# Two model blocks on one core: the second half of a layer as one block and one weight stream, and scatter steps in pairs

## The reference, cut to what matters

```
# end of the recurrent branch, per head of 64
y = (y - mean) * rsqrt(var + RW_GN_EPS) * lnx_g + lnx_b
y = (y + sum(r*k*r_k) * v) * g            # g = sigmoid(gd) @ g_up
# merge, output projection
proj  = einsum('bsgc,gcd->bsgd', branches, w_branch[l])        # 3 x 512 -> 1024
gates = sigmoid(gate_logits)                                   # 1024 -> 3 x 1024
x = x + sum(gates * proj, axis=2) @ w_out[l]                   # 1024 -> 1024
# feed-forward
u = rmsnorm(x, norm2_g[l]) @ ffn_w_up[l]                       # 1024 -> 5632
c = conv_b + sum_j conv_w[j] * shift(u, j)                     # width 3, causal
gate, val = split(c)
x = x + (silu(gate) * val) @ ffn_w_down[l]                     # 2816 -> 1024
```

## Time and profile before

| what | value |
|---|---|
| runs | 3702.34, 3706.68, 3707.23 us; median 3706.68 |
| profiled execution | 3699.1 us, its span 3697.3 us |
| PE busy | 3160.2 us (85%), 20284 instructions |
| weight loads | 2250.0 us (61%) |
| DVE, ACT, POOL busy | 1210.4, 1034.1, 1000.0 us (33%, 28%, 27%) |
| read from HBM | 398.22 MB |
| mean granted clock of TensorE | 0.925 |

### The profile page before, as it was taken

One profiled execution on the slowest core, in us unless ns is written; L12 is line 12 of the kernel. 1 busy time (PEld: TensorE's weight loads), 2 busy tenths in 40 slices (PEclk: granted clock), 3 DMA queues, 4 the chain that ended last, 5 costly groups with the idle time before them and its releaser, 6 DMA issues. The chain is left out here.

```text
span 3697.3 us, 50790 instructions
## 1 busy us (share of the span) xinstructions
PE 3160.2 (85%) x20284; PEld 2250.0 (61%) x20285; DVE 1210.4 (33%) x1819; ACT 1034.1 (28%) x1411; POOL 1000.0 (27%) x560
## 2 busy tenths in 40 slices
PE   6987799879997997979879998386866976999997
PEld 5767766668875776856668876265335855443442
DVE  2175411234401257421224420514652042222222
ACT  3442321144422343232134421221333221111111
POOL 2352123234441353123234442133001521100100
PEclk9998999989998998989999999688888987999998
DMA  3210112122222120012212220120001313898984
GB/s 125 75 57 6 40 69 85 62 81 101 100 94 79 69 74 16 4 71 85 74 70 101 91 105 32 46 80 16 0 23 57 114 40 145 365 394 365 394 358 192
DMA packets 54161, 402.61 MB, mean 109 GB/s; under 512 B 7280, under 2 KB 8432, under 8 KB 14704
## 3 DMA queue, kind: packets, MB, share of 16 engines
q1 hardware_dynamic: 54000, 400.34, 28.0%
HBM read 398.22 MB, written 2.10 MB: 108 GB/s over the span
## 5 line engine op out<-in xcount | busy, mean ns | idle before, releaser
L246 POOL TENSOR_TENSOR w_lo<-w,w_hi 128x1024 fp32r<-128x1024 f32 (+1 forms) x216 | 598.3, 2772 | 1340.3 <-ACT w_hi L241 1340.3
L241 ACT CAST w_hi<-w 128x1024 fp32r<-128x1024 f32 (+1 forms) x216 | 248.7, 1157 | 685.8 <-PE bank L273 647.5
L264 PE MATMUL bank<-h_hi,w_hi 128*128 128x512 f32 x1280 | 349.1, 416 | 63.6 <-ACT w_hi L241 63.6
L264 PEld LDWEIGHTS bank<-h_hi,w_hi 128*128 128x128 f32 x1280 | 244.3, 191 | 144.3 <-ACT w_hi L241 52.0
L273 PE MATMUL bank<-h_hi,w_lo 128*128 128x512 f32 x1280 | 323.0, 394 | 0.0
L269 PE MATMUL bank<-h_lo,w_hi 128*128 128x512 f32 x1280 | 320.1, 393 | 0.0
L269 PEld LDWEIGHTS bank<-h_lo,w_hi 128*128 128x128 f32 x1280 | 241.7, 189 | 54.4
L273 PEld LDWEIGHTS bank<-h_hi,w_lo 128*128 128x128 f32 x1280 | 240.3, 188 | 55.4
L2321 PE MATMUL bank<-moe_w,moe_hg 128*64 128x512 f32 x1024 | 242.5, 601 | 0.8 <-issue 0.8
L573 POOL TENSOR_TENSOR front_w_lo<-w,front_w_hi 128x1024 fp32r<-128x1024 f32 x68 | 167.9, 2472 | 246.4 <-ACT front_w_hi L750 246.4
L1576 DVE TENSOR_TENSOR xT<-xT,bank 128x512 f32 x48 | 33.0, 688 | 394.7 <-PE bank L273 394.7
(11 more groups left out here) (417 smaller groups left out, 5331.2 us busy)
## 6 DMA issues: line engine op xcount, KB each, us to landing
moe_w<-in_moe_w SPq DMA_DIRECT2D x128, 1024.0 KB, 10.8
moe_w<-in_moe_w SPq DMA_DIRECT2D x32, 2048.0 KB, 12.1
w<-in_w_in SPq DMA_DIRECT2D x45, 1024.0 KB, 4.8
w<-in_ffn_up SPq DMA_DIRECT2D x44, 1024.0 KB, 4.8
w<-in_w_merge SPq DMA_DIRECT2D x24, 1536.0 KB, 6.5
w<-in_ffn_down SPq DMA_DIRECT2D x16, 1408.0 KB, 5.9
w<-in_w_out SPq DMA_DIRECT2D x24, 512.0 KB, 3.2
w<-in_w_xk SPq DMA_DIRECT2D x4, 1024.0 KB, 5.9
```

The source lines that it names most:

```text
L241: self.nc.scalar.copy(self.w_hi[:, t, :, :], raw).then_inc(self.sems["w_hi"], 1)
L246: self.nc.gpsimd.tensor_tensor(self.w_lo[:, t, :, :], raw, self.w_hi[:, t, :, :].bitcast(F32), ALU.subtract).then_inc(self.sems["w_lo"], 1)
L264: self.nc.tensor.matmul(bank, hi[:, t, k, :], self.rhs_hi[:, k, 0:self.width], start=(k == 0), stop=False)
```

## The change

The stages from `rwkv_out_phase` to the second `down_phase` become one block, `back_phase`, written out without loops. Its work is numbered as 124 jobs of one split weight tile each: 48 of the merge (a gate tile of depth 8 and a branch tile of depth 4 in turn), 8 of the output projection, 44 of the up projection, 24 of the down projection (each of its 8 tiles in parts of depth 8, 8 and 6). Jobs use the two buffers of `w_hi` and `w_lo` in turn throughout, and 46 chunks of raw weights use the two slots in turn.

- The branch products of the merge are now split like the others: ACT and DVE also split the three branches, and 12 split matmuls replace four unsplit ones per tile. The recurrent branch comes last (`BACK_ORDER`), so its means, variances, gate and scaling run between the first merge tiles.
- `merged` is split tile by tile behind the additions (`high_m`, `low_m`).
- The squares and sums of the second norm run between the tiles of the output projection. The last two tiles of this projection, the norm and the first two up-projection tiles are done in halves of 256 tokens.
- The first two parts of a down tile need only the first 16 of the 22 `made` tiles. The squares and sums for the next norm run between the down tiles, and that norm starts with the roots (`summed=T.ps[6]`). A new `sums_phase` makes the sums of the first norm ahead of the loop.
- 43 semaphores are cleared between layers, 9 before.
- In the experts' stage the scatters of tiles 0 to 5 are issued two at a time, after steps 2, 4 and 6, where one was issued after each of steps 1 to 6.

The parts of the diff that this rests on (`f` is the set of semaphores; `B` holds the buffers):

```diff
@@ norm_phase, sums_phase
+            if summed is None:
+                for k in range(tiles):
+                    nc.scalar.activation(sq[:, k, :], src[:, k, :], ACT.Square).then_inc(sems["squared"], 1)
+                act.wait_ge(sems["summed"], 1)
+            sums = T.ps[0] if summed is None else summed
+            rsqrt(act, sems["rooted"], 0, rstd[:, :], sums[:, 0:width], 1.0 / (tiles * P), T.eps(eps))
...
@@ rwkv_out_phase, merge_phase, ffn_up_phase removed; back_phase added
+GATES, OUTS, UPS, DOWNS, BACK_JOBS = 0, 48, 56, 100, 124
+DOWN_PARTS = ((0, 8), (8, 8), (16, FT - 16))
...
+            for c in range(2, BACK_CHUNKS):
+
+                sync.wait_ge(f["w_lo"], BACK_LAST[c - 2] + 1)
+                fetch(sync, c)
...
+            for n in range(BACK_JOBS):
+                low(n)
+                if n == UPS - 1:
+                    low_h(0)
+                if n == UPS + 1:
+                    low_h(1)
...
+            def gate_and_branch(i):
+
+                bank, b = 2 * (i % 2), BACK_ORDER[i // KD]
+                if i >= 2:
+                    pe.wait_ge(f["added"], i - 1)
+                pe.wait_ge(f["w_hi"], 2 * i + 1)
+                passes(2 * i, T.ps[bank][:, :], *h_tiles, every, True, True).then_inc(f["done"], 1)
+                pe.wait_ge(f["w_hi"], 2 * i + 2)
+                pe.wait_ge(f["y_lo"], 4 * (i // KD) + 4)
+                tiles = [[t[:, k, :] for k in range(y_tiles[b].start, y_tiles[b].stop)] for t in (B.y_hi, B.y_lo)]
+                passes(2 * i + 1, T.ps[bank + 1][:, :], *tiles, every, True, True).then_inc(f["done"], 1)
...
+            means()
+            for i in range(24):
+                gate_and_branch(i)
+                if i == 1:
+                    variances()
+                if i == 3:
+                    out_gates()
+            for m in range(6):
+                out_tile(m)
+                if m:
+                    sum_squares(m - 1)
+            out_half(6, 0)
+            sum_squares(5)
+            out_half(7, 0)
+            sum_half(6, 0)
+            out_half(6, 1)
+            sum_half(7, 0)
+            out_half(7, 1)
+            sum_half(6, 1)
+            up_first(0, 0)
+            sum_half(7, 1)
+            up_first(1, 0)
+            up_first_low(0, 0)
+            up_first_low(1, 0)
+            up_first(0, 1)
+            up_first(1, 1)
+            up_first_low(0, 1).then_inc(f["done"], 1)
+            up_first_low(1, 1).then_inc(f["done"], 1)
+            for j in range(1, FT):
+                for t in range(2):
+                    up_tile(j, t)
+            for m in range(KD):
+                for q in range(3):
+                    down_part(m, q)
+                    if m and q == 0:
+                        sum_next(m - 1)
+            sum_next(KD - 1)
...
+            high(0)
+            high(1)
+            high_y(y_tiles[1])
+            for i in range(24):
+                act.wait_ge(f["done"], 2 * i + 1)
+                high(2 * i + 2)
+                if i >= 2:
+                    act.wait_ge(f["added"], i - 1)
+                nc.scalar.activation(B.sig[:, i % 2, :], T.ps[2 * (i % 2)][:, :], ACT.Sigmoid).then_inc(f["sig_done"], 1)
+                if i == 0:
+                    squares()
+                act.wait_ge(f["done"], 2 * i + 2)
+                high(2 * i + 3)
+                if i == 2:
+                    roots()
+                if i == 4:
+                    high_y(y_tiles[2])
+                if i == 9:
+                    act.wait_ge(f["out_done"], PAIRS)
+                    high_y(y_tiles[0])
+                if i >= 17:
+                    high_m(i - 17)
+            high_m(7)
+            for m in range(6):
+                act.wait_ge(f["done"], OUTS + m + 1)
+                high(OUTS + m + 2)
+                square_x(m, m)
+            square_half(6, 0)
+            square_half(7, 0)
+            root_half(0)
+            square_half(6, 1)
+            act.wait_ge(f["done"], OUTS + 7)
+            high(UPS)
+            high_h(0, (1, 3))
+            act.wait_ge(f["done"], OUTS + 8)
+            high(UPS + 1)
+            high_h(0, (5, 7))
+            square_half(7, 1)
+            root_half(1)
+            high_h(1, (1, 3, 5, 7))
...
+            def norm_half(half):
+
+                cols = halves[half]
+                dve.wait_ge(f["norm_rooted"], 2 * half + 2)
+                if half == 1:
+                    dve.wait_ge(f["h_lo_pool"], KD // 2)
+                    dve.wait_ge(f["h_lo_dve"], KD // 2)
+                for k in range(KD):
+                    nc.vector.scalar_tensor_tensor(out=B.h[:, k, :], in0=xT[:, k, cols], scalar=gain[:, k:k + 1],
+                                                   in1=B.x_rstd[:, cols], op0=ALU.mult, op1=ALU.mult).then_inc(
+                                                       f["normed"], 1)
+                    if k % 2 == 0:
+                        dve.wait_ge(f["normed"], KD * half + k + 1)
+                        nc.vector.tensor_copy(h_hi[:, k, cols], B.h[:, k, :]).then_inc(f["h_hi_dve"], 1)
...
+            add_x(6, halves[1])
+            norm_half(0)
+            dve.wait_ge(f["done"], OUTS + 8)
+            add_x(7, halves[1])
+            norm_half_low(0)
+            norm_half(1)
...
@@ layers
+    sums_phase(nc, T, norm, T.sems["start"], xT)
...
-                rwkv_out_phase(nc, T, rout, rec, R, y_rw, fetch_first(T, merge, 12 * 256, w_merge))
...
+                back_phase(nc, T, back, rec, layer, R, y_ret, y_sg, homes[0], gain("norm2_g"))
...
@@ experts_phase
                     def step(k):
-                        if k == 1:
+                        if k == 2:
                             pe.wait_ge(sems["y_lo"], 2 * g + 2)
-                        if 1 <= k <= 6:
+                        if k in (2, 4, 6):
+                            scatter(g, k - 2)
                             scatter(g, k - 1)
 
```

More of the change, by code:

```diff
@@ L156, with sums_phase, _, norm_phase @@
 NORM_SEMS = "loaded squared summed rooted scaled hi_ready lo_ready"
-def norm_phase(nc, T, sems, stale, src, gain, dst, tiles=KD, width=S, eps=EPS, load=None, ahead=None, parts=None):
+def sums_phase(nc, T, sems, stale, src):
+    with nc.sbuf_tensor([P, KD, S], F32) as sq, nc.Block() as block:
+        @block.sync
+        def _(sync):
+            clear(sync, stale)
+        @block.scalar
+        def _(act):
+            for k in range(KD):
+                nc.scalar.activation(sq[:, k, :], src[:, k, :], ACT.Square).then_inc(sems["squared"], 1)
+        @block.tensor
+        def _(pe):
+            for k in range(KD):
+                pe.wait_ge(sems["squared"], k + 1)
+                nc.tensor.matmul(T.ps[6][:, :], T.ones[:, :], sq[:, k, :], start=(k == 0), stop=(k == KD - 1))
+def norm_phase(nc, T, sems, stale, src, gain, dst, tiles=KD, width=S, eps=EPS, load=None, ahead=None, parts=None,
+               summed=None):
     with nc.sbuf_tensor([P, tiles, width], F32) as sq, nc.sbuf_tensor([P, width], F32) as rstd, \
@@ L1263 @@
 RWKV_REC_SEMS = "masks_loaded right_done right_taken u_done u_taken change_done y_done y_taken state_ready dve"
-def rwkv_out_phase(nc, T, sems, stale, R, out, ahead):
-    col = lambda name, j: T.lc[:, LCOLS[name][0] + j:LCOLS[name][0] + j + 1]
-    with nc.sbuf_tensor([P, 2, S], F32) as sq, nc.sbuf_tensor([P, PAIRS, S], F32) as rstd, \
-            nc.sbuf_tensor([P, RW_W], F32) as up, nc.Block() as block:
+BACK_SEMS = ("w_full*2 w_hi w_lo done clock loaded mean_done centred squared var_done rooted gate_done out_done "
+             "y_hi y_lo sig_done added m_hi m_lo x_added half_done x_squared x_summed norm_rooted normed "
+             "h_hi_act h_hi_dve h_lo_dve h_lo_pool taps_loaded gate_taken val_taken conv_done silu_done made")
@@ L1664, in layers @@
     xT = T.xT
+    sums_phase(nc, T, norm, T.sems["start"], xT)
     with nc.Fori(0, DEPTH) as layer:
+        parts = T.h_hi, T.h_lo
+        chunk = KD * 256
+        gain = lambda name: T.lc[:, LCOLS[name][0]:LCOLS[name][1]]
+        w_in = lambda c: pick(d["w_in"], layer, c)
         with nc.Block() as block:
@@ L1669, in _ @@
             def _(sync):
-                clear(sync, T.sems["start"])
-                clear(sync, down)
+                clear(sync, norm)
+                clear(sync, back)
                 sync.dma_start(T.lc[:, :], pick(d["layer_cols"], layer)).then_inc(head["loaded"], 16)
                 sync.wait_ge(head["loaded"], 16)
-        parts = T.h_hi, T.h_lo
-        gain = lambda name: T.lc[:, LCOLS[name][0]:LCOLS[name][1]]
-        w_in = lambda first: (lambda c: pick(d["w_in"], layer, c + first))
@@ L1710, in layers @@
[L1710 to L1715 removed]
+        norm_phase(nc, T, norm, head, xT, gain("norm1_g"), None, ahead=fetch_first(T, front, chunk, w_in), parts=parts,
+                   summed=T.ps[6])
```

612 lines of the change are left out of this document (378 added, 234 removed).

## The result

The changed kernel takes 3581.01 us, median of four runs (3578.44 to 3584.09), against 3704.51 us for the kernel before on the same chip (3700.94 to 3707.23): a ratio of 0.9668, 95% interval 0.9651 to 0.9684. The prediction was 3584.0 us with a range of 3557 to 3612. The profiled execution has a span of 3581.0 us, where that of before has 3697.3. The rows are rounded, so they add to 116.5.

A forecast was written before the change was run, and what follows sets the result against it. TensorE (PE) was taken as the bound, with waits at weights, norm and split of `merged`. 2 x (-30.2 - 20.3 - 1.8) - 6.4 - 5.7 + 3.5 - 9.5 = -122.7 us gave 3576.4, plus 7.6 for the median: 3584, range 3557 to 3612.

The forecast's parts named there:

- Merge: Merge stage, per layer: split branch products make a tile 8.3 us instead of 8.98, output stage behind tiles; -30.2 us.
- The start: Start of the merge: first chunk lands 6.3 us after issue, PE begins within 9 us of the means, 2 us clock loss.
- Output projection, norm, first pair: Output projection to first up pair, per layer: 97.9 to 77.6 us, 48.7 of it to the first half's sums; -20.3.
- Both predicted waits: Half-tile norm: PE waits for h_hi and for POOL's w_lo, 7 us together in first half, 3 to 4 in second.
- The hand-made schedule: Half-tile norm, followed engine by engine: last scaled half tile after 7.7 us, PE waits for low weights until 11.3.
- the first rival: Overlapped norm runs at the low clock: 12.4 us more a layer than the 3 reckoned, 3609 us; chance 0.11.
- Up: Up projection after its first pair: unchanged, with the same 24 matmuls a tile, casts and convolution; 0 us.
- PE's supply of instructions: Rival, straight-line block: some 115 instruction packets for two layers, 1.15 us each if exposed, 132 us added, 3716; chance 0.03.
- Down: Down projection, per layer: starting wait hidden, 528 products at 0.230 plus seven sums, 129.4 to 127.6 us; -1.8.
- Between the layers and the start: Next root 13.4 us after last matmul instead of 19.8: -6.4, after layer two -5.7; first sums ahead of loop +3.5.
- Experts: Experts' scatters in pairs: 45 changes of matmul kind saved at 0.21 us each, -9.5 us; bounds 0 and 12.
- wins nothing: Rival, norm overlap: POOL's queue and the second half's root chain up, the 20.3 us a layer stay, 3625; chance 0.07.

The follow-up runs named there:

- e2_unsplit: Changed kernel with four unsplit matmuls per merge branch job in place of twelve split ones, casts and waits kept: 3610.52 us.
- The repeat: The changed kernel measured once more, with nothing altered, to see how far its stages repeat: 3583.69 us, ratio 0.9672.
- e4_norm_serial: Changed kernel with both halves' sums and roots first, and PE also waiting for all of h before its first up product: 3600.49 us.
- e3_sums_first: Changed kernel with the sums of both halves and both roots ahead of the first up products; scaling, casts and products stay by halves: 3581.32 us.
- e1_pairs: The kernel before with only the experts' scatters issued in pairs: 3687.47 us, ratio 0.9949.
- e9_rolled_pe: Changed kernel with PE's own program for pairs 3 to 20 of the up projection as a loop: 3581.27 us.

## Why the prediction was right

- **Merge, predicted -30.2, measured -28.0 and -29.3.** The tile is 8.32 for 8.3, and e2_unsplit shows its reason. The start was mis-sized: landing 7.8 us for the 6.3 taken (6.4 before), and 24 first products that lost 2.5 us to the clock where 2 were taken, so PE began 10.2 us after the means, not within 9. The repeat (8.9, and 216.8 for the merge) shows that 1.3 us of this were one transfer's scatter. The waits for `merged` before the output projection are 0.3, not 0.9.
- **Output projection, norm, first pair, predicted 77.6, measured 79.2.** The first part, 48.7 reckoned up to the end of the first half's sums, came out as 710.09 - 661.48 = 48.6. The second was 30.6, not 28.9. Both predicted waits are there, 5.5 us in the first half (7 reckoned) and 2.2 in the second (3 to 4); PE lost 3.8 us to the clock (five passes of eight half products, begun at 722.14, 724.51, 726.58, 734.06 and 735.67, took 8.57 us together, in rhythm 4.75), where 3 were taken, with 0.79 granted where "above 0.8" was asked. The hand-made schedule took DVE and POOL to work side by side: it had the last high part of h after 7.7 us and the low weight part after 11.3, and they came after 8.7 and 12.0. The prediction let the idle time shrink from 27 to 11 and did not say that its 27 are two things: 17.0 us at the norm and 10.0 for the split of `merged`, which goes because the split now runs behind the merge tiles. e4_norm_serial shows that 10 of the 18 us hang on the overlap of the norm, and e3_sums_first that the root by halves isn't needed for them. A granted clock of 0.79 is a mean of both levels: the first rival, bursts that hold the clock low, came true in a small part, 0.8 us a layer beyond what was reckoned.
- **Up, predicted 0, measured +1.2 a layer.** Not PE's supply of instructions; open.
- **Down, predicted -1.8, measured -3.3 and -4.3.** The 0.230 per product was too high; the new block's down projection runs as the old one did, (1099.64 + 1.52 - 974.90 - 7 x 0.885) / 528 = 0.227.
- **Between the layers and the start**, predicted -6.4, -5.7 and +3.5: -7.2, -4.7 and +2.8. The root comes 12.6 us after the last product, 13 were said.
- **Experts, predicted -9.5, measured -15.2.** The term's count (45 changes) was right and its price too small: 0.21 was the scatter's side alone. Two steps in a row take 3.58 where two single ones take 3.74, so the steps carry another 0.16: a step's four products start 0.43 us apart in rhythm, but the first behind a scatter takes 0.48 and the last ahead of one 0.52. The sum's upper end of 12 left this out.
- **The unchanged stages** gave +7.0, predicted 0: 3.8 in block two before the experts, 2.1 from the front matmuls to the means of the two layers, 1.1 at the end. Block two before the experts takes 807.6 us in the profile of before and 809.1 in that of e1_pairs; in the twelve profiles with the new block it takes 807.6 to 817.2, ten of them 811.2 or more. Whether the change adds some 3 us there or it is scatter stays open.
- **Rivals.** The low clock would have needed 12.4 us a layer more, it was 0.8 beyond the 3 reckoned; "wins nothing" is refuted by mid; 34 more packets on q8 came (150 for 116), not 115, and e9_rolled_pe shows no price for them.

Against the terms of the sum, the merge gave 3.1 us less, the norm stretch 3.9, the up projection 2.4 and the unchanged stages 7.0, while the down projection gave 4.0 more and the experts 5.7. These errors partly cancel. And by the profiled executions, from which the terms were worked out, the change is 116.3 us, 6.4 less than the 122.7 predicted; the medians give 123.5 because the profiled execution of before was a fast one. That the forecast of the time came within 3 us is in part luck.

## What to carry to other kernels

Where one engine's work stands between two stages, read which of the others run at once before laying out their schedule: here DVE's instructions lasted up to eight times as long beside POOL's, and moving POOL's work onto DVE, the busier of the two, made the stretch 3.7 us shorter. Before a gain is put down to an overlap, see which waits lie inside the stretch that is compared: more than half of this one's came with the overlap, and the rest with a split that moved out of it. When matmuls of two kinds alternate, price both changes, the one into the short kind and the one back. An overlap has parts that are worth testing apart: the early root earned nothing here, the products under the norm 10 us, and four of them per k another 3.8.

## What was not expected of the hardware

- A cast on DVE of 0.29 us takes 2.32 us, and four subtractions 6.27 for 1.96, while POOL subtracts. DVE makes a low weight part in 1.22 us, POOL in 2.5.
- An experts' up step costs more on both sides of a scatter: its first product behind one takes 0.48 us and its last ahead of one 0.52, where 0.43 is the rhythm.
- After an idle stretch of 4.3 to 7.1 us PE's first 24 products of 512 columns take 7.0 to 8.4 us, without it 6.0; the same 24 take 5.6 in rhythm.
- One 1.5 MB transfer lands 6.1 to 6.3 us after its issue when it is alone (six cases), and 6.2 to 8.4 with a small load just ahead of it and a second large one 0.5 us behind (22 cases).
